# Weight blocks in alternating columns: a fixed byte distance between the two operand streams of TensorE

## Chip, cores, metric

One core of one Trainium2 chip runs the kernel. The metric is the device time of one launch in microseconds (us). Nothing is shared with another core. "ns" is written where a number is in nanoseconds.

## The reference

The reference is three transformer-like layers on 256 tokens (272 with 16 meta tokens in front) of width D = 1024, all in float32. Layer 1 mixes with a gated delta rule (8 heads of 128, chunks of 64), layer 2 with a gated short convolution, layer 3 with a Fourier mix beside a latent attention. Every layer has gated MLPs of hidden width 2816. Almost all of the arithmetic is products of activations with weight matrices:

```python
u, gate = jnp.split(h @ w_up, 2, axis=-1)          # 1024 -> 2 x 2816
u = causal_dwconv(u, conv_w)
return (jax.nn.silu(u) * gate) @ w_down            # 2816 -> 1024
```

Layer 3 has two such MLPs without the convolution, and its shifts, scales and gates come from a product of one vector c with a matrix of 1024 x 9216 ("ada").

## The kernel before

**Split in two parts.** A float32 number x is kept as hi + lo. hi is x rounded to the type fp32r, which TensorE multiplies in one pass, and lo is x - hi, again rounded. A product w * a is then three matmuls that add up in the same PSUM bank: whi * ahi, whi * alo and wlo * ahi. The weights are cut into blocks of 128 x 128 (P = 128) and are the stationary operand, which a LDWEIGHTS instruction puts into the array before each matmul. The activations are the moving operand: 256 to 272 tokens, one column each.

**Units.** A unit is one output tile of 128 rows. In most phases it has KT = 8 blocks, so 24 matmuls. In the phases down0 to down3, an output tile is two units of SLOT_BLOCKS = 11 blocks each. 360 units run in fourteen phases in the order a_in, a_out, up0, down0, b_cx, b_gate, b_out, up1, down1, up2, down2, mix, up3, down3. In down1, down2 and down3 two of the three products are taken in one matmul of 512 columns (L2168, whi times the hi and the lo activations in one bank), and the third (L2169) follows with 256.

**Buffers.** raw, whi and wlo each have SLOTS = 4 slots of 11 blocks (5632 bytes for each partition). Unit u uses slot u % 4. The sync queue loads raw[s] in one DMA (512 KB, 704 KB in down phases) when its last contents have been split. ScalarE makes whi (split_hi, L406), VectorE makes wlo (split_lo, L413), each in one instruction for a whole unit. TensorE waits for lo_split, and for tiles_read, which says that the PSUM bank has been read. So four units may be under way.

**Where the operands lie.** Block k of slot s is the 128 columns whi[:, s, k*P:(k+1)*P]: 512 contiguous bytes in each partition. All buffers start on multiples of 64 bytes. As raw, whi, wlo, hf, xb, hhi and hlo all have sizes that are multiples of 512 bytes, and a slot is 11 * 512, every weight block, and tile 0 of each activation buffer, begin at the same place modulo 512 bytes. Activations hhi and hlo have a pitch of TOK = 272 elements, 1088 bytes, for each k. So tile k lies 64 * k bytes further on, modulo 512. The hidden activations aboth (ahi and alo) have that pitch too. The activations of the mix phase (lhi, llo, uf, fhi, ohi, yhi, ylo) have a pitch of 1024 bytes, and lie at one place modulo 512.

The loop that most matmuls come from (`unit`, L1802 to L1804; `first_step`, L1817, L1818 and L1823, is the same in another order for the first units of a phase):

```python
for k in range(blocks):
    w = slice(k * P, (k + 1) * P)
    nc.tensor.matmul(out, whi[:, s, w], rhi(k0 + k), start=first and k == 0, stop=False)
    nc.tensor.matmul(out, whi[:, s, w], rlo(k0 + k), start=False, stop=False)
    ins = nc.tensor.matmul(out, wlo[:, s, w], rhi(k0 + k), start=False, stop=last and k == blocks - 1)
```

Beside the splits, VectorE reads the finished banks (in up0 and up1 with the convolution, L1421 and L1424; in b_cx L1512 to L1520). In the phases up0 to up1 it also computes the ada products (L1320), one per two units or one per unit, whose matrix the GpSimd queue loads in pieces of 512 KB into a ring of two.

Of the kernel before, what the change touches and what calls it, by code (L numbers as in the profile page):

```python
# [17 lines left out]
LINE = 64  # L18
ARENA = 1291 * LINE
# [68 lines left out]

class Phase:


    def __init__(self, name, first, units, blocks):
        self.name, self.first, self.units, self.blocks = name, first, units, blocks


def plan():
    first, out = 0, []
    for name, units, blocks in [
        ("a_in", 32, KT), ("a_out", 8, KT), ("up0", 2 * FT, KT), ("down0", 16, SLOT_BLOCKS),
        ("b_cx", 16, KT), ("b_gate", 8, KT), ("b_out", 8, KT), ("up1", 2 * FT, KT), ("down1", 16, SLOT_BLOCKS),  # L100
        ("up2", 2 * FT, KT), ("down2", 16, SLOT_BLOCKS), ("mix", 48, KT),
        ("up3", 2 * FT, KT), ("down3", 16, SLOT_BLOCKS),
    ]:
        out.append(Phase(name, first, units, blocks))
        first += units
    return out
# [5 lines left out]
BLOCKS_AFTER = {p.name: q.blocks for p, q in zip(PHASES, PHASES[1:])}  # L112
# [19 lines left out]
X_LAT, X_UF, X_GA, X_Q, X_K, X_V, X_GB, X_GC, X_FO, X_MO, X_OUT = 1, 6, 10, 14, 17, 19, 20, 28, 32, 36, 40  # L132
RHS_AT = {"x": 0, "gdn": 8, "ln0": 16, "ln1": 24, "ln2": 32, "rms0": 40, "rms1": 48, "rms2": 56}
# [33 lines left out]
def build(nc, io):  # L167
    ctx = ExitStack()
    with ctx:
# [18 lines left out]
        wlo = new("wlo", [P, SLOTS, SLOT_BLOCKS * P], F32R)  # L188
        hf = new("hf", [P, KT, TOK])
# [7 lines left out]
        aboth = new("aboth", [P, 2, FT, TOK], F32R)  # L197
# [201 lines left out]
        def split_hi(act, t, s, blocks):  # L399

            if not blocks:
                return
# [3 lines left out]
            nc.scalar.activation(whi[:, s, 0:blocks * P], raw[:, s, 0:blocks * P], ACT.Copy).then_inc(hi_split, 1)  # L406

        def split_lo(dve, t, s, blocks):

            if not blocks:  # L410
                return
            dve.wait_ge(hi_split, t * SLOTS + (s + 1))
            nc.vector.tensor_tensor(wlo[:, s, 0:blocks * P], raw[:, s, 0:blocks * P],  # L413
                                    whi[:, s, 0:blocks * P], ALU.subtract).then_inc(lo_split, 1)

        def steps(eng, phase, body, done=0):
# [3 lines left out]
            after = BLOCKS_AFTER.get(phase.name, 0)  # L420
            whole = n if after == phase.blocks else n - 1
            with eng.Fori(done, whole) as i:
                body(i + t0, i, phase.blocks)
# [2182 lines left out]
```

## Time and profile before

| | |
|---|---|
| median of 3 runs | 1288.32 us (1288.31 to 1289.16) |
| the profiled execution | 1290.6 us |
| its span, first to last instruction | 1288.6 us |
| TensorE busy (PE) | 1259.7 us, 98% of the span |
| VectorE busy (DVE) | 994.6 us, 77% |
| ScalarE busy (ACT) | 686.5 us, 53% |
| from HBM | 242.6 MB, 189 GB/s over the span |

In the rows PE is a matmul and PEld a weight load. Matmuls are pipelined: one record covers the time from its start until its last result, and the next begins long before that ends. So the rate is read from the distance of the starts, called pitch below, and not from the durations. A window of the profile counts the matmuls that touch it, so window length over count gives the mean pitch, and two or three that were in flight at the first edge must be taken off.

### The profile page before, as it was taken

What the parts mean: (1) busy time and instruction counts of PE and PEld (TensorE: products, weight loads), DVE (VectorE), ACT (ScalarE), POOL (GpSimd) and SP (SyncE); (2) the same over time, 40 slices, a digit from 0 to 9 for tenths busy, and PEclk for the clock granted to TensorE, in tenths of its full rate; (3) what the DMA queues carried; (4) which work ended last, traced back from release to release, by engine and by line L of the source; (5) the groups of instructions that cost most, each with busy time, mean ns of one, the idle gap of its engine ahead of it and who ended that gap; (6) DMA issues with size and microseconds to landing.
All of it is one profiled execution on the core that took longest, in us unless ns stands there. A gap on an engine that the chain in (4) does not pass through costs nothing.

```text
span 1288.6 us, 29083 instructions
## 1 busy us (share of the span) xinstructions
PE 1259.7 (98%) x10579; PEld 1212.8 (94%) x10579; DVE 994.6 (77%) x1818; ACT 686.5 (53%) x1117; POOL 55.0 (4%) x93
## 2 busy tenths in 40 slices
PE   9999999999999999999999999999999999999997
PEld 8998898999999999999998899998899999999986
DVE  6897749998979898998877787765666668877654
ACT  6876435655543544655554555553465566655541
POOL 0012000000001010010000000000000000000000
PEclk9999999999999999999999999999999999999999
DMA  7541123688888587488865366665355435666651
GB/s 269 153 127 35 52 83 115 219 302 265 299 278 290 192 299 272 131 307 274 274 232 169 101 209 182 182 210 183 128 179 181 129 104 181 193 181 182 223 178 34
DMA packets 64779, 244.74 MB, mean 190 GB/s; under 512 B 7201, under 2 KB 8513, under 8 KB 64705
## 3 DMA queue, kind: packets, MB, share of 16 engines
q1 hardware_dynamic: 54048, 204.77, 48.9%
q0 software_dynamic: 10656, 38.93, 9.7%
q8 instruction: 52, 0.85, 0.3%
q14 instruction: 23, 0.18, 0.0%
HBM read 242.63 MB, written 1.05 MB: 189 GB/s over the span
## 4 chain that ended last, share of the span: by engine, by line
PE 78%; DVE 4%; issue 1%; ACT 1%; DMA 0%; DVEq 0%; ACTq 0%; POOLq 0%
PE ps L1802 18%; PE ps L1803 18%; PE ps L1804 18%; PE ps L2168 10%; PE ps L2169 5%; PE ps L1817 1%; PE ps L1823 1%; PE ps L1818 1%; PE ps L2313 1%; PE ps L2315 1%; PE ps L2314 1%; DVE wlo L413 1%; DVE xb L1445 1%; PE ps L2218 0%; PE ps L2424 0%
## 5 line engine op out<-in xcount | busy, mean ns | idle before, releaser
L1802 PE MATMUL ps<-hhi,whi 128*128 128x258 f32 (+4 forms) x1952 | 557.2, 285 | 3.5 <-DVE hlo L1050 1.9
L406 ACT ACTIVATE whi<-raw 128x1024 fp32r<-128x1024 f32 (+1 forms) x360 | 400.4, 1113 | 293.1 <-PE ps L1804 167.5
L1803 PE MATMUL ps<-hlo,whi 128*128 128x258 f32 (+4 forms) x1952 | 553.3, 283 | 0.0
L1804 PE MATMUL ps<-hhi,wlo 128*128 128x258 f32 (+4 forms) x1952 | 552.6, 283 | 0.0
L413 DVE TENSOR_TENSOR wlo<-raw,whi 128x1024 fp32r<-128x1024 f32 (+1 forms) x360 | 463.6, 1293 | 87.1 <-ACT whi L406 82.5
L1802 PEld LDWEIGHTS ps<-hhi,whi 128*128 128x128 f32 x1952 | 369.5, 189 | 6.0 <-DVE wlo L413 4.6
L1803 PEld LDWEIGHTS ps<-hlo,whi 128*128 128x128 f32 x1952 | 370.2, 190 | 0.3
L1804 PEld LDWEIGHTS ps<-hhi,wlo 128*128 128x128 f32 x1952 | 370.5, 190 | 0.0
L2168 PE MATMUL ps<-aboth,whi 128*128 128x512 f32 x528 | 186.5, 397 | 0.0
L2169 PE MATMUL ps<-aboth,wlo 128*128 128x256 f32 x528 | 148.2, 281 | 0.0
L2168 PEld LDWEIGHTS ps<-aboth,whi 128*128 128x128 f32 x528 | 99.2, 188 | 23.2
L2169 PEld LDWEIGHTS ps<-aboth,wlo 128*128 128x128 f32 x528 | 99.9, 189 | 0.0
L1320 DVE SCALAR_TENSOR_TENSOR ring<-ring,cb 128x1024 f32<-128x1024 f32 x72 | 87.6, 1218 | 2.7 <-DMA ring<-in_ada_w 2.7
L1802 PE MATMUL ps<-aboth,whi 128*128 128x260 f32 (+1 forms) x240 | 68.4, 285 | 0.3 <-DVE aboth L1533 0.3
L1804 PE MATMUL ps<-aboth,wlo 128*128 128x260 f32 (+1 forms) x240 | 67.8, 283 | 0.0
L1803 PE MATMUL ps<-aboth,whi 128*128 128x260 f32 (+1 forms) x240 | 67.7, 282 | 0.0
L510 POOL DMA_DIRECT2D ring<-in_ada_w x70 | 37.1, 530 | 384.9 <-DVE ring L1320 384.9
L746 ACT ACTIVATE tb<-ps,vec 128x260 f32<-128x260 f32 (+1 forms) x44 | 20.9, 476 | 50.3 <-PE ps L1804 50.1
L1802 PEld LDWEIGHTS ps<-aboth,whi 128*128 128x128 f32 x240 | 45.4, 189 | 0.5 <-DVE aboth L1533 0.5
L1804 PEld LDWEIGHTS ps<-aboth,wlo 128*128 128x128 f32 x240 | 45.3, 189 | 0.0
L1803 PEld LDWEIGHTS ps<-aboth,whi 128*128 128x128 f32 x240 | 45.2, 188 | 0.1
L1817 PE MATMUL ps<-hhi,whi 128*128 128x258 f32 (+3 forms) x160 | 41.0, 294 | 4.1 <-ACT hhi L809 2.4
(419 smaller groups left out, 1560.6 us busy)
## 6 DMA issues: line engine op xcount, KB each, us to landing
raw<-in_w_up SPq DMA_DIRECT2D x176, 512.0 KB, 4.2
raw<-in_w_down SPq DMA_DIRECT2D x64, 704.0 KB, 4.4
ring<-in_ada_w POOLq DMA_DIRECT2D x72, 512.0 KB, 5.1
raw<-in_w_mix SPq DMA_DIRECT2D x48, 512.0 KB, 3.6
raw<-in_w_a_in SPq DMA_DIRECT2D x32, 512.0 KB, 3.6
raw<-in_w_b_cx SPq DMA_DIRECT2D x16, 512.0 KB, 4.7
raw<-in_w_a_out SPq DMA_DIRECT2D x8, 512.0 KB, 3.6
raw<-in_w_b_gate SPq DMA_DIRECT2D x8, 512.0 KB, 4.5
```

The costliest lines, as they stand in the source:

```text
L406: nc.scalar.activation(whi[:, s, 0:blocks * P], raw[:, s, 0:blocks * P], ACT.Copy).then_inc(hi_split, 1)
L413: nc.vector.tensor_tensor(wlo[:, s, 0:blocks * P], raw[:, s, 0:blocks * P], whi[:, s, 0:blocks * P], ALU.subtract).then_inc(lo_split, 1)
L510: pool.dma_start(ring[:, o, :], io["ada_w"][i * 2 + o]).then_inc(ld_ada[o], 16)
L746: nc.scalar.activation(tb[:, p, 0:n], ps[s0][:, 0:n], ACT.Copy, scale=col(j * 3 + taps)).then_inc(f_tap, 1)
L1320: nc.vector.scalar_tensor_tensor(ring[:, r, :], ring[:, r, :], 1.0, cb[:], ALU.mult, ALU.mult, accum_out=small[:, bass.ds(o + 440, 1)]).th ...
L1445: mine(nc.vector.tensor_tensor(xb[:, m, 0:n], xb[:, m, 0:n], ps[6][:, 0:n], ALU.subtract))
L1802: nc.tensor.matmul(out, whi[:, s, w], rhi(k0 + k), start=first and k == 0, stop=False)
L1803: nc.tensor.matmul(out, whi[:, s, w], rlo(k0 + k), start=False, stop=False)
L1804: ins = nc.tensor.matmul(out, wlo[:, s, w], rhi(k0 + k), start=False, stop=last and k == blocks - 1)
L1817: nc.tensor.matmul(ps[s][:, 0:n], whi[:, s, w], hhi[:, k, 0:n], start=k == 0, stop=False)
L2168: nc.tensor.matmul(both, whi[:, s, w], aboth[:, :, h0 + k, 0:SEQ], start=s % 2 == 0 and k == 0, stop=False)
L2169: ins = nc.tensor.matmul(both[:, 0:SEQ], wlo[:, s, w], ahi[:, h0 + k, 0:SEQ], start=False, stop=end)
```

## The change

Three things about the place of data change. The set of instructions, their order and their waits stay, and each matmul multiplies the same numbers.

1. **Weights in pairs.** The host stores each unit with blocks 2j and 2j + 1 woven: column 0 of one, column 0 of the other, column 1 of one, and so on (`paired`). A block is then read with a step of two elements, 8 bytes, over 1024 bytes (`block`). An eleventh block stays contiguous.
2. **Pitch of the pairs.** A slot is described by `Slot(blocks, pitch)`. SPREAD (8 blocks, with hhi and hlo) puts pairs 288 elements = 1152 bytes apart in whi and wlo, so that pair j lies 128 * j bytes further on modulo 512, as tiles 2j of hhi and hlo do. PLAIN and LONG (with activations of a fixed place) keep pairs 1024 bytes apart. The split instructions write and read whi and wlo in four runs of 256 elements for SPREAD, and raw as before.
3. **Distance of the activations.** AHEAD = 128 bytes are put between wlo and hf, so that hhi, hlo and all that lies behind is 128 bytes further on, modulo 512, than the weights. aboth gets a pitch of 3 * P = 384 elements = 1536 bytes, which keeps each of its tiles at that distance.

One unit of mix (X_V) uses its weights as the moving operand. Its weights are not woven.

```diff
+AHEAD = 128
+Slot = namedtuple("Slot", "blocks pitch")
+SPREAD, PLAIN, LONG = Slot(KT, 2 * P + 32), Slot(KT, 2 * P), Slot(SLOT_BLOCKS, 2 * P)
...
         wlo = new("wlo", [P, SLOTS, SLOT_BLOCKS * P], F32R)
+        spot[0] += AHEAD
         hf = new("hf", [P, KT, TOK])
...
-        aboth = new("aboth", [P, 2, FT, TOK], F32R)
+        aboth = new("aboth", [P, 2, FT, 3 * P], F32R)
...
+        def filled(tile, s, slot):
+            if slot.pitch == 2 * P:
+                return tile[:, s, 0:slot.blocks * P]
+            return tile[:, s, 0:slot.blocks // 2 * slot.pitch].rearrange("p (k w) -> p k w", w=slot.pitch)[:, :, 0:2 * P]
...
-            nc.scalar.activation(whi[:, s, 0:blocks * P], raw[:, s, 0:blocks * P], ACT.Copy).then_inc(hi_split, 1)
+            nc.scalar.activation(filled(whi, s, slot), landed(s, slot), ACT.Copy).then_inc(hi_split, 1)
...
-            nc.vector.tensor_tensor(wlo[:, s, 0:blocks * P], raw[:, s, 0:blocks * P],
-                                    whi[:, s, 0:blocks * P], ALU.subtract).then_inc(lo_split, 1)
+            nc.vector.tensor_tensor(filled(wlo, s, slot), landed(s, slot), filled(whi, s, slot), ALU.subtract).then_inc(lo_split, 1)
...
+            def block(tile, s, k, slot, m=P):
+                at_ = k // 2 * slot.pitch
+                if k == slot.blocks - 1 and k % 2 == 0:
+                    return tile[:, s, at_:at_ + m]
+                return tile[:, s, at_:at_ + 2 * m].rearrange("p (w r) -> p w r", r=2)[:, :, k % 2]
...
-                    w = slice(k * P, (k + 1) * P)
-                    nc.tensor.matmul(out, whi[:, s, w], rhi(k0 + k), start=first and k == 0, stop=False)
-                    nc.tensor.matmul(out, whi[:, s, w], rlo(k0 + k), start=False, stop=False)
-                    ins = nc.tensor.matmul(out, wlo[:, s, w], rhi(k0 + k), start=False, stop=last and k == blocks - 1)
+                    nc.tensor.matmul(out, block(whi, s, k, slot), rhi(k0 + k), start=first and k == 0, stop=False)
+                    nc.tensor.matmul(out, block(whi, s, k, slot), rlo(k0 + k), start=False, stop=False)
+                    ins = nc.tensor.matmul(out, block(wlo, s, k, slot), rhi(k0 + k), start=False, stop=last and k == slot.blocks - 1)
...
+def paired(units):
+    n = units.shape[-1] // (2 * P) * 2 * P
+    woven = np.swapaxes(units[..., 0:n].reshape(units.shape[:-1] + (-1, 2, P)), -1, -2)
+    return np.concatenate([woven.reshape(units.shape[:-1] + (n,)), units[..., n:]], -1)
```

## Rows read from the trace of the kernel before

**Rows 1.** The page: busy time by engine, and the chain that ended last.
```profile
PE 1259.7 (98%) x10579; PEld 1212.8 (94%) x10579; DVE 994.6 (77%) x1818; ACT 686.5 (53%) x1117; POOL 55.0 (4%) x93
...
PE 78%; DVE 4%; issue 1%; ACT 1%; DMA 0%; DVEq 0%; ACTq 0%; POOLq 0%
```

**Rows 2.** Windows: PE, PEld, DVE, ACT, POOL busy us; clock; DMA share; GB/s.
```profile
245.00:360.00 115.00, 115.00 (x957) 115.00 (x956) 105.52 (x164) 67.66 (x104) 10.60 (x20) 1.00 0.87 291
370.00:420.00 50.00, 50.00 (x418) 49.94 (x417) 44.41 (x72) 19.07 (x20) 6.78 (x13) 1.00 0.84 292
545.00:655.00 110.00, 110.00 (x922) 110.00 (x921) 100.09 (x158) 63.53 (x99) 10.07 (x19) 1.00 0.88 292
660.00:715.00 55.00, 55.00 (x314) 48.03 (x313) 36.41 (x63) 21.35 (x23) 0.00 (x0) 1.00 0.51 166
```

**Rows 3.** Matmuls by line and form: weights, activations, xcount | busy us, mean ns.
```profile
L1802 PE MATMUL ps<-hhi,whi 128*128 128x258 f32 x992 | 280.2, 283 | 1.1 <-DVE ab L1639 1.0
...
L2168 PE MATMUL ps<-aboth,whi 128*128 128x512 f32 x528 | 186.5, 397 | 0.0
L2169 PE MATMUL ps<-aboth,wlo 128*128 128x256 f32 x528 | 148.2, 281 | 0.0
L1802 PE MATMUL ps<-hhi,whi 128*128 128x262 f32 x432 | 123.7, 286 | 0.0
...
L1802 PE MATMUL ps<-hhi,whi 128*128 128x256 f32 x184 | 52.9, 287 | 0.0
L1802 PE MATMUL ps<-hhi,whi 128*128 128x272 f32 x176 | 52.7, 299 | 1.9 <-DVE hlo L1050 1.9
...
L1802 PE MATMUL ps<-hhi,whi 128*128 128x260 f32 x168 | 47.8, 284 | 0.6 <-DVE wlo L413 0.6
```

**Rows 4.** Weight loads by form: 128, 64 and 96 columns, mean ns of one.
```profile
L1803 PEld LDWEIGHTS ps<-hlo,whi 128*128 128x128 f32 x1952 | 370.2, 190 | 0.3
...
L2005 PEld LDWEIGHTS ps<-gu,ex 64*64 64x64 f32 x332 | 11.7, 134 | 2.1 <-issue 1.1 <-DVE ex L1221 0.7
...
L2313 PEld LDWEIGHTS ps<-lhi,whi 128*96 128x96 f32 x24 | 3.9, 161 | 0.0
```

**Rows 5.** Timeline of TensorE in phase up1: start us, us, engine, line, operation.
```profile
600.89 0.29 PE L1804 MATMUL ps<-hhi,wlo 128*128 128x258 f32 x1
600.89 0.20 PEld L1802 LDWEIGHTS ps<-hhi,whi 128*128 128x128 f32 x1
601.02 0.28 PE L1802 MATMUL ps<-hhi,whi 128*128 128x258 f32 x1
...
601.13 0.28 PE L1803 MATMUL ps<-hlo,whi 128*128 128x258 f32 x1
```

**Rows 6.** Timeline of TensorE in mix: loads of 96 columns, then of 128.
```profile
973.00 0.27 PE L2313 MATMUL ps<-lhi,whi 128*96 128x256 f32 x1
...
974.74 0.28 PE L2313 MATMUL ps<-lhi,whi 128*128 128x256 f32 x1
...
975.10 0.28 PE L2313 MATMUL ps<-lhi,whi 128*128 128x256 f32 x1
```

**Rows 7.** Timeline of TensorE in mix, plain float32 operands.
```profile
998.06 0.59 PE L2384 MATMUL ps<-dft,pf 128*128 128x256 f32 x2
...
1004.53 0.38 PE L2385 MATMUL ps<-dft,pf 128*128 128x256 f32 x1
```

**Rows 8.** Timeline of VectorE in up0 and b_cx; in brackets idle time before.
```profile
292.37 0.49 DVE L1421 SCALAR_TENSOR_TENSOR tb<-ps,vec,tb 128x260 f32<-128x260 f32 x1 [0.48 <-ACT tb L746]
293.01 0.49 DVE L1424 SCALAR_TENSOR_TENSOR tb<-ps,vec,tb 128x260 f32<-128x260 f32 x1 [0.15 <-DVE tb L1421]
...
298.15 0.49 DVE L1421 SCALAR_TENSOR_TENSOR tb<-ps,vec,tb 128x260 f32<-128x260 f32 x1 [0.54 <-ACT tb L746]
...
461.07 0.42 DVE L1512 TENSOR_TENSOR tb<-tb,ps 128x260 f32<-128x260 f32 x1
...
466.36 0.42 DVE L1512 TENSOR_TENSOR tb<-tb,ps 128x260 f32<-128x260 f32 x1
```

More of the change, by code:

```diff
@@ L86, with __init__ @@
 U_V, U_Z = 2 * KT, 3 * KT
+Slot = namedtuple("Slot", "blocks pitch")
+SPREAD, PLAIN, LONG = Slot(KT, 2 * P + 32), Slot(KT, 2 * P), Slot(SLOT_BLOCKS, 2 * P)
 class Phase:
-    def __init__(self, name, first, units, blocks):
-        self.name, self.first, self.units, self.blocks = name, first, units, blocks
+    def __init__(self, name, first, units, slot):
+        self.name, self.first, self.units, self.slot = name, first, units, slot
 def plan():
     first, out = 0, []
[L98 to L102, printed above, removed]
+    for name, units, slot in [
+        ("a_in", 32, SPREAD), ("a_out", 8, SPREAD), ("up0", 2 * FT, SPREAD), ("down0", 16, LONG),
+        ("b_cx", 16, SPREAD), ("b_gate", 8, SPREAD), ("b_out", 8, PLAIN), ("up1", 2 * FT, SPREAD), ("down1", 16, LONG),
+        ("up2", 2 * FT, SPREAD), ("down2", 16, LONG), ("mix", 48, SPREAD),
+        ("up3", 2 * FT, SPREAD), ("down3", 16, LONG),
     ]:
-        out.append(Phase(name, first, units, blocks))
+        out.append(Phase(name, first, units, slot))
         first += units
@@ L760, in act_before_ln @@
                 phase = PH[name]
-                per = 2 if phase.blocks == SLOT_BLOCKS else 1
-                t0, k, after = phase.first // SLOTS, phase.units // SLOTS, BLOCKS_AFTER[name]
+                per = 2 if phase.slot == LONG else 1
+                t0, k, after = phase.first // SLOTS, phase.units // SLOTS, SLOT_AFTER[name]
                 if name != "a_out":
@@ L874, in _, with b_cx @@
             act_ln(1, N_F0, "ln1")
[L876 removed]
+            def b_cx(t, i, slot):
                 for p in range(2):
@@ L1325, in dve_residual @@
                 phase = PH[name]
-                per = 2 if phase.blocks == SLOT_BLOCKS else 1
-                t0, k, after, raw_tiles = phase.first // SLOTS, phase.units // SLOTS, BLOCKS_AFTER[name], RAW_TILES[name]
+                per = 2 if phase.slot == LONG else 1
+                t0, k, after, raw_tiles = phase.first // SLOTS, phase.units // SLOTS, SLOT_AFTER[name], RAW_TILES[name]
                 shift, squares = tb[:, 0, 0:n], sb[:, 0, 0:n]
@@ L1332, in lo_of @@
                 def lo_of(u):
-                    split_lo(dve, t0 + u // SLOTS + 1, u % SLOTS, phase.blocks if u // SLOTS < k - 1 else after)
+                    split_lo(dve, t0 + u // SLOTS + 1, u % SLOTS, phase.slot if u // SLOTS < k - 1 else after)
                 def sum_up(m):
@@ L1659, in _ @@
                 add_squares(4, m)
-            split_lo(dve, PH["up2"].first // SLOTS + 1, 0, KT)
+            split_lo(dve, PH["up2"].first // SLOTS + 1, 0, SPREAD)
             dve_late_norm(4)
@@ L1822, in first_step @@
                             pe.wait_ge(rhs_ready, RHS_AT[version] + k + 1)
-                        ins = nc.tensor.matmul(ps[s][:, 0:n], whi[:, s, k * P:(k + 1) * P], hlo[:, k, 0:n], start=False, stop=k == KT - 1)
+                        ins = nc.tensor.matmul(ps[s][:, 0:n], block(whi, s, k, SPREAD), hlo[:, k, 0:n], start=False, stop=k == KT - 1)
                     ins.then_inc(unit_done, 1)
@@ L1866, in _ @@
                     for k in range(KT):
-                        nc.tensor.matmul(ps[u][:, 0:TOK], whi[:, u, k * P:(k + 1) * P], r[:, k, 0:TOK], start=r is hhi and k == 0, stop=False)
+                        nc.tensor.matmul(ps[u][:, 0:TOK], block(whi, u, k, SPREAD), r[:, k, 0:TOK], start=r is hhi and k == 0, stop=False)
                 pe.wait_ge(lo_split, u + 1)
                 for k in range(KT):
-                    last = nc.tensor.matmul(ps[u][:, 0:TOK], wlo[:, u, k * P:(k + 1) * P], hhi[:, k, 0:TOK], start=False, stop=k == KT - 1)
+                    last = nc.tensor.matmul(ps[u][:, 0:TOK], block(wlo, u, k, SPREAD), hhi[:, k, 0:TOK], start=False, stop=k == KT - 1)
                 last.then_inc(unit_done, 1)
@@ L2546, in lay_out @@
     mixing_layout(a, f)
+    for p in PHASES:
+        units = f["w_" + p.name]
+        f["w_" + p.name] = paired(units) if p.name != "mix" else np.concatenate([paired(units[:X_V]), units[X_V:X_V + 1], paired(units[X_V + 1:])])
     return {k_: np.ascontiguousarray(v_) for k_, v_ in f.items()}
```

168 lines of the change are left out of this document (85 added, 83 removed).

## The prediction

> **What bounds the kernel now.** I read the page first. TensorE is busy for 1259.7 of 1288.6 us, and the chain that ended last is PE for 78%, nothing else above 4% [rows 1]. That says who is on the path, not how fast it works, so I took the pitch next: windows inside one phase, where PE is busy for the whole window. Phase up1 (258 columns) has 922 matmuls in 110 us, 119.6 ns each after the three in flight at the edge are taken off. Up0 (262 columns) has 957 in 115 us, 120.5 ns. Down0 (260 columns) has 418 in 50 us, 120.5 ns. Down1 has 314 in 55 us, two of which belong to a column sum, so 156 pairs of 512 and 256 columns, 352.6 ns a pair [rows 2].
>
> What should a matmul take? The granted clock is 1.00 in all of these windows, its level of 2.4 GHz. At one column per cycle 258 columns are 107.5 ns. Matmuls on plain float32 give a clean yardstick: 31 passes start 6.47 us apart from first to last [rows 7], 30 steps of 215.7 ns for 256 columns. That is two cycles per column (213.3 ns) and 2.4 ns more. So I take 2.4 ns as the fixed part. The expected pitch is then 109.9 ns for 258 columns, 111.6 for 262, 110.7 for 260, and 109.1 + 215.7 = 324.8 for a pair of down1. Above it remain 9.7, 8.9, 9.8, and 27.8 ns a pair. Nothing waits in these windows, so TensorE loses 8% of its time inside its own instruction stream.
>
> The weight load isn't itself the bound. It starts with the matmul before [rows 5]. Loads of 64, 96 and 128 columns last 134, 161 and 190 ns [rows 4], so 0.84 to 0.91 ns for one column beside a constant: a load that streams needs about 107 to 112 ns for 128 columns, and is hidden under the matmul.
>
> **Where the lost time comes from.** Three rows bear on it. First, in mix the same activations (lhi, llo, 256 columns) are met by loads of 96 and then of 128 columns: 15 steps from 973.00 to 974.74 are 116.0 ns each, 3 steps from 974.74 to 975.10 are 120.0 ns [rows 6]. Only the load differs, so the excess over 109.1 ns, 6.9 against 10.9 ns, comes with the load. Second, in rows 7 there is no excess though the loads have 128 columns. There the activations go by at one column in two cycles, 4 bytes in 0.83 ns, the speed at which a weight load goes through its 512 bytes. For fp32r the activations go twice as fast as the weights, so that the distance of the two addresses changes by 512 bytes in each load. Third, within one phase the pitch isn't constant: 0.13 us and then 0.11 us between neighbours of one form [rows 5], with nothing but the addresses different. I read from this that the two reads disturb each other when their addresses stand at certain distances, and that each fp32r load passes through such distances.
>
> The Trainium skill speaks against this reading ("TensorE: Matmul & The Clock Gate", section "Step-by-step: what each phase is for"): TensorE has two independent read ports, and loading the next weights takes no read bandwidth from the running matmul. Rows 6 don't agree. By the rule alone nothing would change and the sum would be zero.
>
> **The change part by part.**
> Weaving: a weight read with a step of 8 bytes passes through 1024 bytes in the same time, the speed of the fp32r activations. The distance now stays what it was at the start. With AHEAD it starts at 128 bytes modulo 512 in down, and in mix's own buffers. In the SPREAD units it is 128 for an even k (the next load is in the same pair), and for odd k 192 within a pair and 64 at the step to the next. If the bad distances lie around zero, all of these are clear of them.
> The gain where it is full: outside down1 to down3 there are some 7,560 such matmuls (248 units of 24 outside mix, 46 in it, 16 of 33 in down0; rows 3 show 1,952 of them, those of L1802 on hhi, each with its two companions). At the mean of the three excesses, 9.5 ns, they give 71.8 us. 528 pairs [rows 3] at 27.8 ns give 14.7 us. Together 86.5 us. Below this bound nothing can go unless the fixed part shrinks too.
> What I take off: (a) no row shows equal speeds for fp32r, nor whether distances of 64 and 192 bytes are clear. The bounds are an excess of 0 and of 9.5 ns. I take 1 ns per matmul, 8.6 us, nearer the zero of rows 7, since they are the only ones with equal speeds. (b) In the gated delta rule, units fill gaps between dependent steps. A dozen of 24 matmuls give little there, 3 us. (c) VectorE. In up0 its cycle of two units is 5.78 us with 0.54 us idle [rows 8], so it needs 5.24. TensorE will need 48 x 111.6 ns = 5.36. In b_cx it already runs with no idle time at 5.29 us, and TensorE comes down to 48 x 110.7 = 5.31. So VectorE stays just ahead, by 2% and by less than 1%, and a lag at the start of a phase is no longer made good. I take 3 us in all for waits on wlo. If all of up0, b_cx and up1 were held at VectorE's pace it would cost no more, for the paces are equal.
> Splits: four runs of 256 in place of one of 1024, same elements. The profile has no such form. Bounds are 0 and, if each further run cost as much as the idle time between two dependent instructions (0.15 us) [rows 8], 3 x 0.15 us a split. I take 0; at the upper end VectorE's cycle in up0 and up1 grows by 0.9 us to 6.1. VectorE then sets the pace, 0.8 us behind TensorE's in each of 44 cycles, and 35 us of the gain are gone (1251 us).
> The 128 bytes and the wider aboth: addresses only. DMAs: same number and bytes.
> Sum: -86.5 + 8.6 + 3 + 3 = -71.9 us. From the profiled 1290.6 (span 1288.6) that is 1218.7. The median stands 2.3 us below the profiled execution, so the time is **1216 us**.
>
> **The rivals.**
> *A, slower: the strided read is dearer.* The excess comes with each piece of memory that a weight load opens, and the woven block lies over twice as many bytes. For it: the excess falls with the load's columns [rows 6], 6.9 to 10.9, near 96 to 128. Against it: the pitch varies with the address [rows 5], and rows 7 have full loads at no excess. Excess doubled: 1288 + 86 = 1374 us. It decides once the woven pitch is above 120 ns. The extreme is a load at half speed, 213 + 2.4 ns each: (216 - 120) x 8,616 = 827 us more. Nothing in the rows points there.
> The Trainium skill has the threshold ("Advanced Engine Details and Errata", section "SBUF Cachelines"): lines of 16 bytes, and at least two accesses to each for full speed. A step of 8 bytes has just two, so by it the load pays nothing. No row shows a strided load.
> *B, no change.* The excess isn't from the meeting of the two reads, but from the fp32r stream alone. For it: at 512 columns, where a load covers half of the time, the pair's excess is 27.8 ns and not twice 9.5. Against it: rows 6. Time 1288 us. This is also what the Trainium skill's two-port rule gives.
> *C, partial.* The bad distances are wide, and 64 or 192 bytes fall in them. The half of the SPREAD matmuls with odd k then keeps its excess, and a read that starts later than its record says would move the pattern in the same way. For it: rows 4 give each load a constant of some 80 ns, of which I can't tell where it lies. Half of the sum: -36 us, 1252 us.
> *D, another engine takes over.* VectorE as above, or the DMAs: in the streams they move 291 GB/s at a share of 0.87 [rows 2]. At 8% less time that is 315 GB/s at 0.94. If they stop at a 5% gain, the 330 us from up0 to up1 lose some 10 us: 1226 us. The slack of a slot (one iteration of four units, 11 us) speaks against it.
>
> **How the numbers follow.** Forecast, with D in it, 1200 to 1232: 0.58. C, 1232 to 1285: 0.22. Full gain with no loss, below 1200: 0.04. B: 0.04. A: 0.12. The range 1198 to 1262 takes in the forecast with D, the bound of 86.5 us less what (b) and (c) must cost, and most of C, about 8 in 10. The forecast's own range is 1200 to 1232. A difference of 0.2% (2.6 us) is about what three runs can tell from none. Faster is 0.58 + 0.22 + 0.04 = 0.84, same 0.04, slower 0.12.
>
> **What would show it.** Right: about 990 matmuls in 110 us of up1 or up2 (111 ns), some 337 in 55 us of down1 in place of 314, neighbours 0.11 us apart throughout, and the 96 and 128 column loads of mix at one pitch. Weight load records stay near 190 ns. Split records stay near 1.06 and 1.22 us. VectorE's idle time before L1421 in up0 goes to almost nothing, and its share of the span rises to 82%. Wrong: a pitch near 120 again (B), one that alternates with k between 110 and 120 (C), load records longer than 200 ns and a pitch above 120 (A), or PE waits on wlo of more than 10 us in all with a pitch of 111 (D).

## The result, and the profile after

The changed kernel takes **1304.47 us** (median of 4 runs, 1304.11 to 1305.29), the kernel before beside it 1288.32 us (4 runs). The ratio is 1.0123, 95% interval 1.011 to 1.0136: slower by 16 us, where 1216 us had been predicted. Slower was rival A, with a chance of 0.12, but the loss is a fifth of its price.

The page of the kernel after, the lines that answer to [rows 1]:

```profile
span 1302.6 us, 29013 instructions
...
PE 1273.8 (98%) x10579; PEld 1230.5 (94%) x10579; DVE 997.2 (77%) x1818; ACT 686.2 (53%) x1117; POOL 54.7 (4%) x93
...
PE 88%; DVE 7%; ACT 2%; issue 1%; DMA 1%; SPq 0%; DVEq 0%; ACTq 0%
```

PE's busy time grew by 14.1 us and the span by 14.0. The time is in TensorE's own stream. The same stretches of phases as in [rows 2], by windows (PE, PEld, DVE, ACT, POOL busy; clock; DMA share; GB/s):

```profile
245.00:360.00 115.00, 115.00 (x937) 115.00 (x937) 104.21 (x161) 65.36 (x101) 10.56 (x20) 1.00 0.86 284
372.50:422.50 50.00, 50.00 (x413) 49.95 (x412) 43.69 (x70) 18.85 (x20) 6.42 (x13) 1.00 0.85 290
550.00:660.00 110.00, 110.00 (x899) 110.00 (x898) 98.53 (x155) 61.55 (x96) 10.04 (x19) 1.00 0.85 284
667.00:722.00 55.00, 55.00 (x313) 48.85 (x312) 36.03 (x63) 20.98 (x22) 0.00 (x0) 1.00 0.50 161
```

Read as before, with three in flight taken off, up0 (262 columns) has a pitch of 123.1 ns (before 120.5), down0 (260) 122.0 (120.5), up1 (258) 122.8 (119.6), and a pair of down1 takes 353.7 (352.6; nothing is taken off for pairs in either). The granted clock is 1.00 in all, the level of 2.4 GHz. Some 3,360 matmuls of 258 columns at 3.2 ns more, 1,440 of 262 at 2.6, 1,104 of 260 at 1.5 and 528 pairs at 1.1 are 10.8 + 3.7 + 1.7 + 0.6 = 16.8 us (an estimate: all phases of one width are put at the window's pitch). That covers the whole loss. Added up from start to start over both traces, the matmuls with streamed weights take 14.6 us more, where the span grew by 14.0.

Weight loads and splits by line and form, kernel after; the loads answer to [rows 4]:

```profile
L1831 PEld LDWEIGHTS ps<-hlo,whi 128*128 128x128 f32 x1952 | 388.2, 199 | 0.2
...
L2195 PEld LDWEIGHTS ps<-aboth,wlo 128*128 128x128 f32 x528 | 103.7, 196 | 0.0
```
```profile
L436 DVE TENSOR_TENSOR wlo<-raw,whi 128x1024 fp32r<-128x1024 f32 x296 | 361.4, 1222 | 83.0 <-ACT whi L429 78.7
```

A load's record went from 190 to 199 ns, in the down phases to 196. VectorE's split still takes 1222 ns, and ScalarE's 1056 (1055 before), so four runs of 256 cost nothing, as the prediction had it. Timeline of TensorE in up1, kernel after, beside [rows 5]:

```profile
600.30 0.29 PE L1830 MATMUL ps<-hhi,whi 128*128 128x258 f32 x1
600.42 0.29 PE L1831 MATMUL ps<-hlo,whi 128*128 128x258 f32 x1
600.55 0.29 PE L1832 MATMUL ps<-hhi,wlo 128*128 128x258 f32 x1
600.67 0.29 PE L1830 MATMUL ps<-hhi,whi 128*128 128x258 f32 x1
```

The steps are 0.12 and 0.13 us: none is the 0.11 that was forecast.

### The profile page after: what moved, and what is told of

It reads as the page before. It is cut to its first block, busy times and chain, and to the rows that moved or that the text cites. A ratio compares the mean times of both kernels' runs of the same rounds, so it can differ in the third digit from the quotient of the medians.

```text
span 1302.6 us, 29013 instructions
## 1 busy us (share of the span) xinstructions
PE 1273.8 (98%) x10579; PEld 1230.5 (94%) x10579; DVE 997.2 (77%) x1818; ACT 686.2 (53%) x1117; POOL 54.7 (4%) x93
## 4 chain that ended last, share of the span: by engine, by line
PE 88%; DVE 7%; ACT 2%; issue 1%; DMA 1%; SPq 0%; DVEq 0%; ACTq 0%
PE ps L1832 19%; PE ps L1830 19%; PE ps L1831 19%; PE ps L2194 10%; PE ps L2195 5%; DVE wlo L436 2%; DVE tb L1125 2%; PE ps L1844 2%; PE ps L1850 2%; PE ps L1845 1%; PE ps L2339 1%; PE ps L2340 1%; PE ps L2341 1%; PE ps L2054 1%; DMA raw<-in_w_a_in 1%
## 5 line engine op out<-in xcount | busy, mean ns | idle before, releaser
L1832 PE MATMUL ps<-hhi,wlo 128*128 128x258 f32 (+4 forms) x1952 | 560.1, 287 | 0.0
L1830 PEld LDWEIGHTS ps<-hhi,whi 128*128 128x128 f32 x1952 | 385.8, 198 | 4.8 <-DVE wlo L436 3.3
L1831 PEld LDWEIGHTS ps<-hlo,whi 128*128 128x128 f32 x1952 | 388.2, 199 | 0.2
L1832 PEld LDWEIGHTS ps<-hhi,wlo 128*128 128x128 f32 x1952 | 384.4, 197 | 0.0
L2194 PEld LDWEIGHTS ps<-aboth,whi 128*128 128x128 f32 x528 | 103.4, 196 | 20.5
L2195 PEld LDWEIGHTS ps<-aboth,wlo 128*128 128x128 f32 x528 | 103.7, 196 | 0.0
L1830 PEld LDWEIGHTS ps<-aboth,whi 128*128 128x128 f32 x240 | 47.0, 196 | 0.5 <-DVE aboth L1555 0.4
L1831 PEld LDWEIGHTS ps<-aboth,whi 128*128 128x128 f32 x240 | 47.0, 196 | 0.0
L1832 PEld LDWEIGHTS ps<-aboth,wlo 128*128 128x128 f32 x240 | 47.0, 196 | 0.0
```

Of the source, the lines that this page charges most:

```text
L1830: nc.tensor.matmul(out, block(whi, s, k, slot), rhi(k0 + k), start=first and k == 0, stop=False)
L1831: nc.tensor.matmul(out, block(whi, s, k, slot), rlo(k0 + k), start=False, stop=False)
L1832: ins = nc.tensor.matmul(out, block(wlo, s, k, slot), rhi(k0 + k), start=False, stop=last and k == slot.blocks - 1)
L2194: nc.tensor.matmul(both, block(whi, s, k, LONG), aboth[:, :, h0 + k, 0:SEQ], start=s % 2 == 0 and k == 0, stop=False)
L2195: ins = nc.tensor.matmul(both[:, 0:SEQ], block(wlo, s, k, LONG), ahi[:, h0 + k, 0:SEQ], start=False, stop=end)
```

## The experiments

Theories at the start: the forecast's (two reads that meet, distance decides), a dearer strided load, an excess that belongs to the fp32r stream alone, and other engines. "Train" below means a row of equal matmuls back to back, which computes nothing of the reference. Its pitch is the distance between the starts of the steady part, over the number of steps. The diffs of the trains are written short: each line stands for many trains of that kind.

**1. trains1: one suspected term at a time.** 47 trains of 80 matmuls.

```diff
-for _ in range(80): matmul(out, w[:, 0:128], a[:, 0:256])               # contiguous, distance 0
+for _ in range(80): matmul(out, w[:, 0:128], a[:, d:d + 256])           # other distances d
+for _ in range(80): matmul(out, woven(w, 2), a[:, d:d + 256])           # weights with a step of 8 bytes (4: 16 bytes)
+for _ in range(80): matmul(out, w[:, 0:1].to_broadcast([P, 128]), ...)  # a load that stands still; the same for a
```

> This kernel computes nothing of the reference: TensorE runs 45 trains of 80 equal matmuls on fixed operands, each train on a source line of its own, and the output is a copy of a weight block. The pitch of each train is read from the timeline. Theory 1 (the two reads disturb each other at certain distances of their addresses): for fp32r, 256 columns and a woven load, the pitch depends on the distance; some distances give 109 to 110 ns, others well over 125; with contiguous loads it is near 120 at every distance, as in the kernel before; still operands (step 0) have no excess or a constant one. Theory 2 (each piece of memory that a load opens costs the activations something, wherever it lies): the pitch doesn't depend on the distance; about 120 ns contiguous, 123 to 126 woven, more with a step of four, and it falls with the number of load columns. Theory 3 (the disturbance is by other engines or DMAs): 109 ns in all quiet trains, and 120 only in those beside a busy VectorE, ScalarE or DMA.

Its timeline; a train is one row, and the start of the next row less its own start, over 80, is its pitch. L298, L301 and L307 are contiguous at 256, 320 and 448 bytes from the weights' start, L310 and L313 woven at 0 and 64, L343 has the step of 16 bytes, L394 a load that stands still, L406 bf16:

```profile
57.67 9.74 PE L298 MATMUL ps<-a,w 128*128 128x256 f32 x80
67.25 9.59 PE L301 MATMUL ps<-a,w 128*128 128x256 f32 x80
...
86.17 9.26 PE L307 MATMUL ps<-a,w 128*128 128x256 f32 x80
95.27 9.76 PE L310 MATMUL ps<-a,w 128*128 128x256 f32 x80
104.87 9.76 PE L313 MATMUL ps<-a,w 128*128 128x256 f32 x80
...
201.15 18.84 PE L343 MATMUL ps<-a,w 128*128 128x256 f32 x80
219.82 18.83 PE L346 MATMUL ps<-a,w 128*128 128x256 f32 x80
...
410.48 9.25 PE L394 MATMUL ps<-a,w 128*128 128x256 f32 x80
419.56 9.12 PE L397 MATMUL ps<-a,w 128*128 128x256 f32 x80
...
465.25 8.93 PE L406 MATMUL ps<-ab,wb 128*128 128x256 bf16 x80
473.93 9.83 PE L409 MATMUL ps<-a,w 128*128 128x256 f32 x80
```

Contiguous, the distance does matter: 119.9 ns at 0 and 256 bytes, 117.8 at 64, 118.6 at 128, 113.4 at 192 and 448. Woven, it hardly does: 120.0 to 121.0 at eleven distances, never less. The step of 16 bytes gives 233.3. Beside activations at distance 0, a still load gives 113.4, and still activations 112.0. Loads of 32, 64 and 96 columns give 117.8, 113.3 and 116.0: no line through these. Trains with VectorE, ScalarE or a DMA busy beside them gave 119.9 to 120.0 contiguous and 121.1 woven, as without them, so theory 3 is out at these loads (VectorE busy for 8.0 of 9.0 us, ScalarE for 6.7, the DMA at a share of 0.53). Neither of the others came out as written: theory 1 had the distance matter for woven loads and not for contiguous ones, and it is the other way round; theory 2 had no distance matter.

**2 to 5. One part of the change each, in the whole kernel.** ahead_only is the kernel before with the 128 bytes alone. The others are the kernel after: woven_only has weaving and the old places, dist_zero loses the 128 bytes alone, and unwoven has the changed places and contiguous blocks, nothing woven by the host.

```diff
# ahead_only, against before
+        spot[0] += 128                                             # ahead of hf
# woven_only, against after
-AHEAD = 128
-SPREAD, ... = Slot(KT, 2 * P + 32), ...
-        aboth = new("aboth", [P, 2, FT, 3 * P], F32R)
+AHEAD = 0
+SPREAD, ... = Slot(KT, 2 * P), ...
+        aboth = new("aboth", [P, 2, FT, TOK], F32R)
# dist_zero, against after
-AHEAD = 128
+AHEAD = 0
# unwoven, against after (and the host leaves the blocks as they are)
-                return tile[:, s, at_:at_ + 2 * m].rearrange("p (w r) -> p w r", r=2)[:, :, k % 2]
+                return tile[:, s, at_ + k % 2 * P:at_ + k % 2 * P + m]
```

> The kernel before with 128 bytes between wlo and hf, nothing else. Theory 1: each contiguous load sweeps 512 bytes of distance whatever the start, so within 0.3% of before (1286 to 1291 us). Theory 2: no change at all. If the time rises by some 16 us, the distance and not the weaving is what made the changed kernel slower.

> The changed kernel with weaving alone: all pairs 1024 bytes apart, no 128 bytes, aboth at its old pitch. Distances start at 0 to 448 bytes. Theory 1: the distances are now mixed, some of them bad for a whole load, so slower than the changed kernel if 64 to 192 are good ones, by 1% or more. Theory 2: the same as the changed kernel, 1304 us.

> The changed kernel with AHEAD = 0, so that the distances are 0 and 64 (or 448) bytes in place of 128, 192 and 64. Theory 1: clearly other than 1304 us (slower by 2% or more if zero is the bad distance, faster if 128 is). Theory 2: 1304 us, within 0.2%.

> The changed kernel with every block contiguous again (and the host's weaving left out), but its places kept: pairs 1152 bytes apart, activations 128 bytes on, aboth at 1536 bytes. If the weaving alone makes the changed kernel slower (theory 4), this is at the kernel before or a little under it: the distances are then 128, 192 and 64 bytes in place of an even mix of four, 118.6, 113.4 and 117.8 ns in the first trains against a mean of 117.4, so 1280 to 1292 us. If the places make it slower, it stays near 1304 us.

| kernel | us | ratio to before, 95% | us against before |
|---|---|---|---|
| ahead_only | 1288.65 | 0.9997 (0.9987 to 1.0006) | 0 |
| woven_only | 1300.63 | 1.009 (1.0073 to 1.0107) | +11.8 |
| dist_zero | 1300.15 | 1.0088 (1.0071 to 1.0104) | +11.3 |
| unwoven | 1296.52 | 1.0054 (1.0038 to 1.0071) | +6.9 |

Up1 in unwoven, the window and a load's record:

```profile
549.00:659.00 110.00, 110.00 (x899) 110.00 (x898) 98.56 (x153) 60.74 (x96) 10.02 (x19) 1.00 0.85 282
```
```profile
L1831 PEld LDWEIGHTS ps<-hlo,whi 128*128 128x128 f32 x1952 | 371.9, 191 | 0.3
```

The changed places alone bring up1 to 122.8 ns with loads of 191 ns. Weaving alone costs 12 us. So both halves of the change lose time, each by itself, and they don't add up (11.8 + 6.9 against 16). Of the expectations only that for ahead_only was met. woven_only is 0.3% faster than the changed kernel, where one theory had it slower by 1% and the other the same, and dist_zero is 0.3% faster too, far from the one theory's 2% and outside the other's 0.2%. unwoven was to be at 1280 to 1292 us if weaving alone did the harm, and near 1304 if the places did: 1296.5 is between, and both do.

ahead_only says less than it seems to. The tiles of hhi, hlo and aboth lie 64 bytes further for each k, so they stand at all multiples of 64 modulo 512 before and after the shift, in another order. Only the mix phase's own buffers came to a new place.

**6 to 8. trains2, trains3, trains4: scanning the places.** trains2 has 76 trains of 60 matmuls by start of the activations. trains3 has the layouts of a whole unit (24 matmuls with their pitches, three times over) and trains4 the same at every 4 bytes.

```diff
+            ins = [nc.tensor.matmul(ps[0][:, 0:258], wt(r, k, 0, 512), ac(r, k, 258, 1088, 28), ...)
+                   for _ in range(3) for k in range(8) for r in range(3)][-1]   # start 28 bytes further
```

> Again nothing of the reference is computed: 76 trains of 60 equal fp32r matmuls. Contiguous loads of 128 columns against 256, 258, 260, 262 and 272 columns and against two runs of 256 (as in down1), each at distances of 0 to 240 bytes modulo 256; then loads of a still address (step 0) against 128 to 512 columns; then woven loads against 258 and 512. Theory 4 (a fp32r activation stream costs 17 cycles for 16 columns whatever is loaded, and a contiguous load adds up to 7 ns by the distance modulo 256): the still loads give 113.3 ns at 256, 114.2 at 258, 226.7 at 512; contiguous loads at 258 columns vary with the distance between 114 and 122 and are best near 192; woven loads are 120 to 124 at each distance. Theory 2 (each opened piece costs the same): no dependence on the distance. My own reading in the prediction: woven loads have at least one distance with 110 ns.

> Nothing of the reference is computed. 108 layouts are run by themselves: three units of 24 matmuls each, in the order of a unit (whi on hi, whi on lo, wlo on hi, for k = 0 to 7) with the addresses that the layout gives them, and 19 layouts of the 512 and 256 column pairs; nothing else runs. Theory 5 (the pitch follows from the types, the columns and the addresses alone, nothing outside TensorE): the layouts of the three kernels give their pitches of the real runs, 258 columns: before 119.8, changed 122.8, contiguous in the changed places 122.4; pairs before 352, changed 355. Some layout with an activation pitch of 1280 bytes is below 118 at 258 columns. Theory 3 (other engines matter): all layouts are near each other and below the real ones. Six trains at the end: bf16 operands give 109.9 ns at 258 columns and 215.8 at 512, so that the whole excess belongs to fp32r; loads of 32 columns still leave 225 ns or more at 512 (the excess isn't the load's); still activations give 215.8 at 512 (it is the moving of the activations).

> Layouts by themselves once more, contiguous loads only, to choose a start of the activations to the element: 116 layouts of a unit and 7 of the pairs. Theory 5 (pitch from types, columns and addresses): the layout of the kernel before with its activations 16 bytes on gives 118.0 ns at 258 columns as in the last trains, neighbours of 4 bytes differ by up to 2 ns, none is below 113.3 ns (the pitch with a still load), and no layout is best for all of 256, 258, 260, 262 and 272 columns. If the pitch were set by the distance in steps of 64 bytes alone, all starts from 0 to 60 would be alike.

trains2: with a load that stands still, 113.3 ns at 256 columns, 116.7 at 258, 124.7 at 272 and 231.7 at 512. With a moving one, 258 columns take 117.4 to 122.1 by the start, 256 take 113.3 at starts of 112 and 192 bytes and 116.7 to 120 elsewhere. Woven 258: 123.4, 122.4 and 120.0. So theory 4 was right on still loads at 256 columns and on woven ones, and wrong on still loads at 258 and 512 (114.2 and 226.7 expected) and on the best start for 258 columns (192 bytes give 120.9).

512 columns with a moving load at distance 0 (L333), then 258 and 512 columns with a still load (L353, L359):

```profile
425.42 13.81 PE L333 MATMUL ps<-a,w 128*128 128x512 f32 x60
...
550.38 7.16 PE L353 MATMUL ps<-a,w 128*128 128x258 f32 x60
...
575.37 14.06 PE L359 MATMUL ps<-a,w 128*128 128x512 f32 x60
```

At 512 columns the still load is no help: 231.7 ns, against 227.1 to 234.3 with a moving one.

trains3 rebuilds the kernels' pitches with nothing else running. At 258 columns the layout of before gives 119.6, that of after 122.7, contiguous blocks in the changed places 122.4, woven blocks in the old places 121.8. The pair gives 349.1 in the old layout, 355.4 in the changed one, 351.3 with contiguous blocks there (the expectations below have 351.4 and 346.9 for trains of pairs, each some 2.4 ns too high, because 24 of the 47 steps they were read from are the long ones of 512 columns). So no other engine is needed for these numbers, though the pair's step of 6 ns overstates the kernel's of 1 to 2. At 258 columns most layouts with another pitch or start stay within 118 to 122, and no rule of bad distances around zero came out of them. None with a pitch of 1280 bytes is below 118, where one had been expected.

The last trains of trains3 take the operands apart: a load of 32 columns at 258 (L365) and 512 (L367) columns of activations, then still activations at 512 (L369):

```profile
1205.78 7.42 PE L365 MATMUL ps<-lo,whi 128*32 128x258 f32 x60
1213.04 14.06 PE L367 MATMUL ps<-lo,whi 128*32 128x512 f32 x60
1226.94 13.28 PE L369 MATMUL ps<-lo,whi 128*128 128x512 f32 x60
```

That is 117.8, 231.7 and 218.7 ns. At 512 columns neither a still load nor one of a quarter of the columns takes the excess away (231.7 both), and still activations take 13 ns of it. bf16 operands take 110.0 ns at 258 columns and 216 at 512, with no excess over the yardstick.

trains4: the start modulo 16 bytes decides several ns. At 258 columns a start of 4 bytes gives 121.2, 8 gives 119.5, 16 gives 117.7, 28 gives 117.1, 36 gives 121.1, 60 gives 117.8. Neighbours of 4 bytes differ by up to 3 ns, where 2 were expected. Two windows of it, the start of 4 and the start of 28 bytes (PE, PEld, ACT, POOL busy; clock; DMA share; GB/s):

```profile
173.00:181.00 8.00, 8.00 (x68) 8.00 (x67) 0.00 (x0) 0.00 (x0) 1.00 0.00 0
225.00:232.90 7.90, 7.90 (x70) 7.90 (x69) 0.00 (x0) 0.00 (x0) 1.00 0.01 2
```

One layout (blocks 576 bytes apart, start 176) gave 116.1 in trains3 and 120.5 in trains4, steadily in both and with the buffers at the same addresses, so the pitch isn't a function of the addresses alone.

**9 and 10. start_28 and placed: contiguous weights, activations moved.** If only the place counts, a better one must beat the kernel before.

```diff
 # start_28, against before
-        hhi = new("hhi", [P, KT, TOK], F32R)
-        hlo = new("hlo", [P, KT, TOK], F32R)
+        rows = lambda flat, first, k, n: flat[:, first:first + k * n].rearrange("p (k n) -> p k n", n=n)
+        hh = new("hh", [P, 2 * KT * TOK + 64], F32R)
+        hhi, hlo = rows(hh, 7, KT, TOK), rows(hh, 7 + KT * TOK, KT, TOK)      # 28 bytes; sqb likewise
 # placed, against start_28
-        aboth = new("aboth", [P, 2, FT, TOK], F32R)
+        both_rows = new("both_rows", [P, 2 * FT * 320 + 64], F32R)
+        aboth = both_rows[:, 7:7 + 2 * FT * 320].rearrange("p (h k n) -> p h k n", h=2, n=320)
-        spot[0] = arena                                            # the mix phase's own buffers
+        spot[0] = arena + 192
```

> The kernel before with one edit: the high and low rows that the streamed units read start 28 bytes further, so that each block's activations are read 28 bytes past its weights modulo 64; weights stay contiguous, and the 256-byte step of everything behind stays. If the pitch of a matmul is set by where its activation words lie, trains of this layout said 117.1 ns at 258 columns in place of 119.6, 118.9 at 260, 120.0 at 262 in place of 120.6, 125.0 at 272: 2.5 ns on some 3,360 matmuls of 258 columns, 0.7 on 1,440 of 262 and 0.5 on 1,104 of 260, about 10 us in all, so 1278 us (1274 to 1283). If the trains' differences belong to trains alone (one layout gave 116.1 in one kernel of trains and 120.5 in another), the kernel stays at 1288 us and its pitch at 119.8 to 119.9.

> As the run before, and the rest of the rows placed as well: the rows of the down stages get a pitch of 1280 bytes in place of 1088 and start 28 bytes past the weights, and the mixing stage's own rows (pitch 1024) lie 192 bytes past the weights modulo 256. Trains of these layouts said 346.9 ns a pair in place of 351.4 (528 pairs: 2.4 us) and 113.3 ns at 256 columns in place of 120.0 (some 350 matmuls: 2.3 us). If placing is what counts and not a weight's order in memory: another 4 to 5 us, 1273 us (1268 to 1280). If trains say nothing for the whole kernel: 1288 us.

start_28 takes **1279.53 us**, ratio 0.9929 (0.9915 to 0.9942). placed takes **1272.34 us**, ratio 0.9875 (0.986 to 0.989), the fastest of all here. Both are within what was expected. Windows of placed in up0, up1, down1 and the last units of mix:

```profile
245.00:358.00 113.00, 113.00 (x945) 113.00 (x943) 104.41 (x162) 66.06 (x102) 10.57 (x20) 1.00 0.87 293
...
544.00:649.00 105.00, 105.00 (x898) 105.00 (x898) 97.51 (x156) 61.17 (x95) 10.03 (x19) 1.00 0.87 296
656.00:708.00 52.00, 52.00 (x303) 45.73 (x302) 34.70 (x62) 20.78 (x21) 0.00 (x0) 1.00 0.52 170
```
```profile
1054.00:1074.00 20.00, 20.00 (x179) 20.00 (x178) 18.11 (x31) 12.96 (x23) 0.00 (x0) 1.00 0.59 179
```

Up1 takes 105 / 895 = 117.3 ns a matmul (trains4: 117.1), up0 120.0, a pair of down1 345.5 with two of a column sum taken off. From start to start, without the column sum, a pair takes 344.4 (trains4: 344.4), and 351.7 in the kernel before. The matmuls on yhi and ylo in mix start 113.4 ns apart on average; in the kernel before they start exactly 120 apart, in the kernel after 121.1.

**11. placed_woven: weaving in the best places.** placed, with weights woven and pairs 1024 bytes apart.

> The fastest kernel so far (activations placed 28 and 192 bytes past the weights, hidden rows with a pitch of 1280 bytes, 1272.3 us) with one edit: the weights of all units but one are stored in alternating columns and read with a step of 8 bytes, pairs 1024 bytes apart. If weaving costs something by itself, whatever the place of the activations: all trains of woven loads took 120.0 ns and more at 256 and 258 columns, so up1 and up2 go from 117.2 back to 120 to 122 ns, the mixing stage's own from 113.3 to 120, and the time is 1292 us (1285 to 1300). If weaving cost time in the earlier runs only because the places were bad for it: within 3 us of 1272 us. If a fixed distance brings the gain that was predicted once the place is a good one: below 1265 us.

**1300.4 us**, ratio 1.0088 (1.0074 to 1.0102): the first of the three cases, and at the upper end of its range. Up1 is back at 121.4 ns. Mix's last units, the window that answers to the last one above: 120.0 ns between starts on average.

```profile
1076.00:1096.00 20.00, 20.00 (x169) 20.00 (x168) 17.30 (x31) 12.38 (x21) 0.00 (x0) 1.00 0.58 182
```

With all whole-kernel runs side by side:

| us | places of before | changed places | placed |
|---|---|---|---|
| contiguous | 1288.5 | 1296.5 | 1272.3 |
| woven | 1300.6 | 1304.5 | 1300.4 |

(Each was run beside the kernel before, whose median moved between 1288.3 and 1289.6; unwoven is 6.9 us above its own.) Contiguous kernels differ by some 23 us with the place, woven ones by 4. Something keeps the woven ones at 120 ns and above in all three sets of places.

**12. trains5: how long does the load take by itself?** Activations stand still, or are few, so that the load alone can set the pitch.

```diff
+for _ in range(60): matmul(out[:, 0:n], w[:, 0:128], a[:, 0:1].to_broadcast([P, n]))      # n = 64 ... 272
+for _ in range(60): matmul(out[:, 0:n], woven(w, 2, m), a[:, 0:1].to_broadcast([P, n]))   # m = 96 ... 128
+for _ in range(60): matmul(out[:, 0:n], woven(w, 4, m), a[:, 0:1].to_broadcast([P, n]))
```

> Trains of 60 equal matmuls each, which compute nothing of the reference, at the full clock: weight loads contiguous, with a step of 8 bytes and of 16 bytes, against activations that stand still (one column repeated) or move, with 64 to 272 columns of activations and 96 to 128 columns of weights. The question is why a woven load never came below 120 ns. Theory 1, the load alone takes that long: 128 columns of weights with a step of 8 bytes take 120 ns of their own reading, so still activations and short ones (64 and 128 columns) leave the woven trains at 118 to 121 ns where contiguous ones give 112, fewer columns of weights lower it in proportion (some 0.9 ns a column), and the step of 16 bytes stays at 233 even with 64 columns of activations. Theory 2, the woven load disturbs the activations' reading: with still or short activations the woven trains come down to 112 to 113 ns like contiguous ones, and only moving activations of 240 columns and more bring 120.

Timeline, trains of 60, activations standing still but in L291. Contiguous loads first, woven ones from L247, the step of 16 bytes in L265, a woven load against 240 moving columns in L291, then woven loads of 120 and 128 columns. The granted clock is 1.00 in all but L227 and L259, where it is 0.50:

```profile
43.68 13.04 PE L227 MATMUL ps<-a,w 128*128 128x128 f32 x60
...
65.69 6.88 PE L231 MATMUL ps<-a,w 128*128 128x224 f32 x60
72.40 6.87 PE L233 MATMUL ps<-a,w 128*128 128x240 f32 x60
79.11 6.89 PE L235 MATMUL ps<-a,w 128*128 128x256 f32 x60
85.84 6.96 PE L237 MATMUL ps<-a,w 128*128 128x258 f32 x60
92.64 7.28 PE L239 MATMUL ps<-a,w 128*128 128x272 f32 x60
...
133.16 7.24 PE L247 MATMUL ps<-a,w 128*128 128x224 f32 x60
140.24 7.24 PE L249 MATMUL ps<-a,w 128*128 128x240 f32 x60
147.31 7.24 PE L251 MATMUL ps<-a,w 128*128 128x256 f32 x60
154.38 7.23 PE L253 MATMUL ps<-a,w 128*128 128x258 f32 x60
161.45 7.29 PE L255 MATMUL ps<-a,w 128*128 128x272 f32 x60
...
182.49 14.24 PE L259 MATMUL ps<-a,w 128*128 128x128 f32 x60
...
224.55 14.17 PE L265 MATMUL ps<-a,w 128*128 128x240 f32 x60
238.56 14.17 PE L267 MATMUL ps<-a,w 128*128 128x256 f32 x60
...
363.03 7.37 PE L291 MATMUL ps<-a,w 128*128 128x240 f32 x60
...
494.01 6.88 PE L319 MATMUL ps<-a,w 128*120 128x256 f32 x60
500.73 7.23 PE L321 MATMUL ps<-a,w 128*128 128x256 f32 x60
```

Contiguous, the pitch stays at 111.7 ns for 224 and 240 columns, and rises from there: 112.0, 113.3 and 118.7 at 256, 258 and 272. Woven, it stays at 117.8 for 224, 240, 256 and 258, and reaches 118.7 at 272. With the step of 16 bytes it is 233.3 at 240 to 272 columns. A flat stretch means that the columns of activations don't set the pace, and it moves with how the weights are read, so it is put down to the load: 128 columns take 111.7 ns contiguous, 117.8 woven and 233.3 with a step of 16 bytes. With 120 woven columns in place of 128 the train takes 112.0, so there it is the load that sets the pace. For contiguous loads no train with few activation columns has fewer columns of weights. What is shown is that at a clock of 1.00 no train of fp32r matmuls with loads of 128 columns came below 111.6: trains1 has 111.7 with 128 moving columns too (L370), where bf16 takes 55.8 (trains5, L343).

Theory 1 is right for the 117.8. It isn't all: woven loads against 240 moving columns take 120.0 (L291), against 112.0 contiguous, so moving activations add another 2 ns, which is theory 2's part. The trains with 64, 128 and 192 columns of activations ran partly or wholly at a granted clock of 0.50 and can't be read against these.

## Why the prediction was wrong

**What bounds the kernel: half right.** TensorE's own stream sets the end, all of the difference is in its pitch, and D and the splits were seen rightly: no other engine moved. "The weight load isn't itself the bound ... and is hidden under the matmul" is where it went wrong first. The estimate of 107 to 112 ns came from durations of records with 64, 96 and 128 columns. The measured 111.7 is its upper end, and that lies above the 109.9 ns which the forecast took as the new pitch at 258 columns. By that floor no change of distance could have reached it. (The pair's 352.6 was a little high as well: nothing in flight was taken off; start to start it is 351.7.)

**The yardstick of 2.4 ns: wrong for fp32r.** It came from float32 passes [rows 7]. With still activations an fp32r matmul takes 113.3 ns at 258 columns, 5.8 above 107.5, and 112.0 at 256, 5.3 above 106.7. bf16 takes 109.2 at 256, 2.5 above. So some 3 ns of each "lost" 9.5 are there with activations that stand still, an estimated 25 of the 86.5 us.

**The failed step: "Where the lost time comes from", with the term for weaving that follows from it.** It says that the two reads meet, that equal speed holds them at one distance, and that the excess is then gone. At 256 columns its first half holds: with both moving a matmul takes 119.9 ns at distance 0, with a still load 113.4, with still activations 112.0, and a contiguous load goes from 119.9 to 113.4 with the start of the activations. At 258 columns a still load leaves 116.7, and at 512 it takes nothing away (231.7), so the meeting of the two reads isn't the whole excess. The second half doesn't hold. A read with a step of 8 bytes does not go "through 1024 bytes in the same time": it takes 6.1 ns longer, 117.8, and this alone puts a floor under every woven matmul. In place of the forecast's excess of 1 ns (term a), 120.0 to 123.4 ns were measured at 256 and 258 columns at every distance tried, 2 to 6 ns above that floor. The floor explains why the gain could not come. It lies below the 119.6 ns of before, so it doesn't by itself explain why woven kernels are 12 us slower; what makes the 2 to 6 ns above it is not shown. Terms (b) and (c) were never put to the test, as there was no gain for them to eat. Rows 6, the main evidence, misled. In trains of 256 columns of activations at distance 0, loads of 32, 64, 96, 104, 112, 120 and 128 columns give 117.8, 113.3, 116.0, 118.7, 113.3, 117.3 and 119.9: the pitch goes up and down, and two points of it looked like a slope. Rows 7 had another type, at another speed.

The Trainium skill's rule of two independent read ports ("TensorE: Matmul & The Clock Gate", section "Step-by-step: what each phase is for") was rightly doubted: with the matmul unchanged, a load that stands still in place of one that moves is worth 6.5 ns at 256 columns (113.4 against 119.9, trains1). At 512 columns it is worth nothing (231.7 against 227.1).

**The price of a strided read: rival A's claim, at a smaller size.** A put the point of decision at a woven pitch above 120 ns, and 122.8 came; its other sign, load records longer than 200 ns, was just missed at 199. Its price, the excess doubled, was too high: the strided load costs 6.1 ns of its own, and that is hidden where the matmul takes longer (118.7 at 272 still columns, woven or not). In woven_only, 312 matmuls of down1 took 54.96 us, against 54.95 before.

The rule in the Trainium skill ("Advanced Engine Details and Errata", section "SBUF Cachelines") asks for two accesses to each 16 bytes. The drop behind that point agrees (233.3 ns with one access to a line), but two accesses were not free: 117.8 against 111.7.

**The places: taken as free, and cost 7 us by themselves.** Unwoven blocks in the changed places give 122.4 in trains and 122.8 in the kernel against 119.6. "If the bad distances lie around zero" had nothing behind it: in trains2 contiguous blocks at 64, 128 and 192 bytes took 119.1, 122.1 and 120.9 ns at 258 columns, against 121.0 at 0.

**C and B.** C's pitch that alternates between 110 and 120 didn't come. B had more of the truth than its chance of 0.04 says, though not its time: of 9.7 ns above the 109.9 of 258 columns, 3.4 are there with still activations (113.3), 6.8 with a still load (116.7), and at 512 columns the whole excess is there with a load of 32 columns (231.7 against bf16's 216).

**Open.** Whether it is the distance of the two reads that counts or the address of the activations alone (the trains never moved the weights by themselves), why the start modulo 16 bytes counts when the weights are at a multiple of 64, why a distance of 192 is good at 256 columns and not at 258, why one layout gave two pitches, what holds woven matmuls 2 to 6 ns above their floor, and whether some place would bring them down to 117.8. No run here separates these.

## What to carry to other kernels

Before costing a change of an operand's layout, measure the load by itself: a train of matmuls whose activations stand still, with a few column counts below the one in use. A flat stretch that moves with the weights' layout is the load's own time, and here it was within 2 ns of what 256 and 258 columns take with still activations. Then let each operand stand still in turn, at more than one column count, before the excess is put down to their meeting. Two pitches from a trace are not a slope, and where addresses are in play a scan is needed; one small kernel holds some seventy trains. Steps that are long and short by turns are read over whole periods. Then try places with the data as it is: moving rows by 28 and 192 bytes and one pitch from 1088 to 1280 gave 16 us (1272.3 against 1288.5), and no instruction changed its work.

## What the runs showed of the hardware

- fp32r matmuls whose load has 128 columns come no closer than 111.7 ns at a granted clock of 1.00 (trains5, 224 and 240 still columns; trains1, 128 moving ones), 117.8 with a step of 8 bytes in the load and 233.3 with 16. At a granted clock of 0.50 (trains5) the step of 16 bytes took 233.3 too (L259), so that read doesn't follow TensorE's clock. Contiguous (L227) and woven (L243) both took 213.3 there.
- Activations with a step of 8 bytes cost far more than weights with one: 230.0 ns at 256 columns in trains1 (L400).
- With contiguous loads the pitch of 256 columns goes from 113.3 to 120.0 with the start of the activations in equal matmuls (trains2, steps of 16 bytes), and from 117.2 to 121.9 in whole units (trains4, steps of 4 bytes). bf16 stays at 109.2 whether its load is contiguous (trains1) or has a step of 4 bytes, two elements (trains5).
- At 512 columns an fp32r matmul takes 231.7 ns with a still load or one of 32 columns, and 218.7 with still activations; bf16 takes 216 (trains2, trains3).
